# A hybrid decoder step on one core: normed rows kept in the operands' own buffers, all three thirds normed before the operand differences, and half of the down rows' low parts moved to VectorE

## The reference

```
hp = rms_norm(xp, norm_ffn[layer])
z = h @ w_up                      # 1024 -> 2 x 2816
g, u = split(z)
g_c, new_prev = causal_dwconv(g, prev, conv_w)        # width 3
xp = xp + (silu(g_c + conv_b) * u) @ w_down           # 2816 -> 1024
```

## Time and profile before

| | |
|---|---|
| median of 3 runs | 2657.35 us (2650.94 to 2659.35) |
| profiled execution | 2655.65 us |
| its span (first to last instruction) | 2653.9 us |
| mean granted TensorE clock | 0.967 of full speed |

### The profile page before, as it was taken

How to read it: one execution, slowest core, us unless ns; L and a number is a source line. 1 busy time by engine, 2 the same in 40 slices (tenths; PEclk the granted TensorE clock), 3 DMA queues, 4 the chain that set the end, 5 groups by cost and what they waited for, 6 DMA issues and landing times. The chain is left out here.

```text
span 2653.9 us, 43480 instructions
## 1 busy us (share of the span) xinstructions
PE 2478.8 (93%) x17818; PEld 2359.4 (89%) x17818; DVE 1532.3 (58%) x1863; ACT 823.7 (31%) x1304; POOL 1116.4 (42%) x752
## 2 busy tenths in 40 slices
PE   5999978999889999999999999879889999999997
PEld 4999955659889999999998999869889999999997
DVE  5988976533686666664447303172686666654446
ACT  4311144542343333332113322221343333332111
POOL 3766641002265555554443212252265555554441
PEclk9999988999989999999999999989989999999998
DMA  3887779993022222233220212312012322233221
GB/s 145 285 299 256 256 273 321 331 335 120 25 64 72 95 74 73 83 118 115 91 84 33 108 40 60 135 50 101 25 64 72 97 72 73 89 120 106 89 72 64
DMA packets 135185, 330.69 MB, mean 125 GB/s; under 512 B 21157, under 2 KB 25126, under 8 KB 134474
## 3 DMA queue, kind: packets, MB, share of 16 engines
q1 hardware_dynamic: 110634, 259.30, 28.4%
q10 hardware_dynamic: 24064, 67.56, 7.6%
q0 software_dynamic: 288, 1.05, 0.1%
HBM read 284.52 MB, written 43.32 MB: 124 GB/s over the span
## 5 line engine op out<-in xcount | busy, mean ns | idle before, releaser
L1396 PE MATMUL PS<-OP,OPW 128*128 128x258 f32 x7056 | 854.7, 284 | 18.8 <-DVE GUP L2633 7.4
L1396 PEld LDWEIGHTS PS<-OP,OPW 128*128 128x128 f32 x7056 | 853.1, 191 | 20.3 <-issue 15.2
L1031 PE MATMUL G<-HHI,WHI 128*128 128x344 f32 x2496 | 726.4, 323 | 23.7 <-POOL WLO L2843 12.1
L1031 PE MATMUL G<-HHI,WLO 128*128 128x344 f32 x2016 | 648.1, 321 | 0.0
L1031 PE MATMUL G<-HLO,WHI 128*128 128x344 f32 x1536 | 493.0, 321 | 0.0
L1031 PEld LDWEIGHTS G<-HHI,WHI 128*128 128x128 f32 x2496 | 460.0, 190 | 27.1 <-issue 26.3
L2843 POOL TENSOR_TENSOR WLO<-WRAW,WHI 128x1024 fp32r<-128x1024 f32 x94 | 231.5, 2469 | 563.9 <-ACT WHI L1636 563.8
L2505 DVE TENSOR_TENSOR XT<-XT,G 128x1032 f32<-128x1032 f32 x172 | 211.4, 1229 | 354.4 <-PE G L1031 354.1
L1031 PEld LDWEIGHTS G<-HHI,WLO 128*128 128x128 f32 x2016 | 382.6, 190 | 0.0
L2921 POOL TENSOR_TENSOR OPW<-WRAW,OPW 128x512 fp32r<-128x512 f32 x200 | 279.0, 1400 | 205.7 <-ACT OPW L1949 205.7
L1031 PEld LDWEIGHTS G<-HLO,WHI 128*128 128x128 f32 x1536 | 291.0, 189 | 0.3
(11 more groups left out here) (365 smaller groups left out, 3388.6 us busy)
## 6 DMA issues: line engine op xcount, KB each, us to landing
XT<-in_ck SPq DMA_DIRECT2D x256, 256.0 KB, 4.7
WRAW<-in_w ACTq DMA_DIRECT2D x108, 512.0 KB, 3.7
HF<-in_cv SPq DMA_DIRECT2D x176, 256.0 KB, 4.8
WRAW<-in_w SPq DMA_DIRECT2D x60, 512.0 KB, 4.0
hidden_rows<-HRB SPq DMA_DIRECT2D x44, 516.0 KB, 6.2
VTOK<-hidden_rows SPq DMA_DIRECT2D x22, 1032.0 KB, 4.9
XT<-in_cv SPq DMA_DIRECT2D x80, 256.0 KB, 4.5
SPARE<-in_w SPq DMA_DIRECT2D x22, 512.0 KB, 5.4
```

Of the source, the lines that this page charges most:

```text
L1031: mm = pe.matmul(out[:, c], w, x[:, c * TC:(c + 1) * TC], start=first and n == 0, stop=last and n == 2)
L1396: mm = pe.matmul(out[:, q * PIECE:(q + 1) * PIECE], w[:, at], v, start=starts and c == 0 and r == 0, stop=ends and c == 3 and r == 2, skip ...
```

## The change

1. `HNB` goes. Each normed row is written where later a difference is formed in place (`RAW1`, `RAW2`), so that all thirds can be held. For the middle third its place is in four runs, and `normed` writes it by two instructions of 172 columns instead of one of 344.
2. VectorE norms all three thirds first and then forms the differences (`operand_add`, in place, order T1, T3, T2, T4), between the weight sums. `conv_gate(0)` comes ahead of the low part of T1's last third, and all low parts of T4 after that.
3. ScalarE: GATE's copy no longer waits for the last difference, but the high parts of T2 now stand ahead of it; the copies of pair 1's P2 and P5 and the high parts of T3 stand ahead of SiLU 0, and the high parts of P4 and P7 behind it. GpSimd: all its low parts of third 1 ahead of P1's; the states of pair 0 ahead of P3's low part, T3's low parts ahead of P4's.
4. At the end of the pairs, ScalarE loads down unit 1 with unit 0 and rounds both together; GpSimd makes both units' low parts (unit 1's after P6 of the last pair) before the hidden rows.
5. VectorE makes the low part of every chunk's second hidden row (`second_low`): chunk 0's ahead of the last `conv_gate`, chunk c + 1's behind tile 3 of chunk c. GpSimd keeps the first rows. TensorE and SyncE wait for both counters.

Squares use another buffer (`SQ_FRONT`), and two semaphores are merged; neither adds a wait that is not there before.

```
         def normed_raw(n, b, c):
-            return HNB[:, c] if n % 2 else third(HN[c % 4], b)
+            if n % 2 == 0:
+                return third(HN[c % 4], b)
+            raw, size, apart = (RAW1, RAW1_SIZE, LOWER) if c < 4 else (RAW2, RAW2_SIZE, OPERAND)
...
+                    if n % 2 and b == 1:
+                        STT(out=out[:, 0], in0=x[:, 0], scalar=gain, in1=scale[:, 0], op0=ALU.mult, op1=ALU.mult)
+                        out, x, scale = out[:, 1], x[:, 1], scale[:, 1]
...
                 invert(n, 1)
-                operand_adds(n, 0)
                 normed(n, 1, 0, 4)
                 invert(n, 2)
                 normed(n, 1, 4, ND)
-                operand_adds(n, 1)
+                normed(n, 2)
+                operand_add(layer, X_T1, 0)
+                operand_add(layer, X_T1, 1)
                 weight_sum(layer, 1, S1)
+                operand_add(layer, X_T1, 2)
                 weight_sum(layer, 1, S3)
-                operand_low(layer, X_T4, 0)
-                normed(n, 2)
-                operand_adds(n, 2)
+                for x in (X_T3, X_T2, X_T4):
+                    operand_add(layer, x, 0)
                 operand_low(layer, X_T1, 0)
...
+                operand_low(layer, X_T1, 1)
...
                 weight_sum(layer, 1, S2)
                 weight_sum(layer, 1, S4)
...
+                conv_gate(0)
                 operand_low(layer, X_T1, 2)
-                conv_gate(0)
+                operand_low(layer, X_T4, 0)
...
+                def second_low(c):
+
+                    dve.wait_ge(hid_hi, layer * NF + 2 * c + 2)
+                    xhi, xlo = down_parts(c)
+                    TT(xlo[:, 1], HRAW[c % 2][:, 1], xhi[:, 1].bitcast(F32), ALU.subtract).then_inc(hid_lo_dve, 1)
...
+                    if p == NF - 1:
+                        second_low(0)
                     conv_gate(p)
...
                         add_tile(td + 8 * c, m, None)
+                        if m == 3:
+                            second_low(c + 1)
...
                 act.wait_ge(tile_done, tp + 2)
-                act.wait_ge(t_added, adds_count(layer, 2, X_T3))
                 A(by3(GATE), psum_tile(tp), ACT.Copy).then_inc(tile_free[tp % 2], 1)
-                turned_to_high(layer, 7, 8)
                 A(by3(HRB[:]), psum_tile(tp + 1), ACT.Copy).then_inc(tile_free[(tp + 1) % 2], 1)
+                turned_to_high(layer, 5, 6)
                 op_high(layer, 1, P6)
                 op_high(layer, 1, P3)
-                turned_to_high(layer, 8, 9)
+                turned_to_high(layer, 6, 9)
+                copy_product(1, P2)
+                turned_to_high(layer, 9, 11)
+                copy_product(1, P5)
+                turned_to_high(layer, 11, 12)
                 silu(0)
                 op_high(layer, 1, P4)
...
                         low(ud)
+                        pool.wait_ge(product_done, product_count(layer, p, P6))
+                        low(ud + 1)
                         hidden(0)
-                        low(ud + 1)
```

More of the change, by code:

```diff
@@ L1996, in mlp @@
                 act.wait_ge(tile_done, tp + 2)
-                act.wait_ge(t_added, adds_count(layer, 2, X_T3))
                 A(by3(GATE), psum_tile(tp), ACT.Copy).then_inc(tile_free[tp % 2], 1)
-                turned_to_high(layer, 7, 8)
                 A(by3(HRB[:]), psum_tile(tp + 1), ACT.Copy).then_inc(tile_free[(tp + 1) % 2], 1)
+                turned_to_high(layer, 5, 6)
                 op_high(layer, 1, P6)
                 op_high(layer, 1, P3)
-                turned_to_high(layer, 8, 9)
+                turned_to_high(layer, 6, 9)
[3 more added lines that the diff above has]
+                turned_to_high(layer, 11, 12)
                 silu(0)
                 op_high(layer, 1, P4)
[L2006 to L2012, removed]
+                op_high(layer, 1, P7)
+                op_high(layer, 2, P1)
+                op_high(layer, 2, P2)
+                for p in range(1, NF - 1):
+                    if p > 1:
                         op_high(layer, p + 1, P1)
@@ L2015, in mlp @@
                         op_high(layer, p + 1, P2)
[L2016 to L2043, removed]
+                        copy_product(p, P5)
+                    op_high(layer, p + 1, P5)
+                    op_high(layer, p + 1, P6)
+                    copy_product(p, P3)
+                    op_high(layer, p + 1, P3)
+                    copy_product(p, P4)
+                    op_high(layer, p + 1, P4)
+                    silu(p)
+                    op_high(layer, p + 1, P7)
+                p = NF - 1
+                act.wait_ge(op_lo_ready, product_count(layer, p - 1, P7))
+                load(ud)
+                load(ud + 1)
+                copy_product(p, P2)
+                copy_product(p, P5)
+                act.wait_ge(op_lo_ready, product_count(layer, p, P7))
+                load(ud + 2)
+                high(ud)
+                high(ud + 1)
+                copy_product(p, P3)
+                hidden(0)
+                copy_product(p, P4)
+                high(ud + 2)
+                load(ud + 3)
+                silu(p)
+                load(ud + 4)
                 for c in range(FI - 1):
@@ L2950, in mlp @@
                 n = 2 * layer + 1
-                pool.wait_ge(h_lo_pool, max(count for (m, b, c), (on, count) in LOWS.items() if m == n and on))
-                pool.wait_ge(h_lo_dve, max(count for (m, b, c), (on, count) in LOWS.items() if m == n and not on))
-                pool.wait_ge(t_added, adds_count(layer, 2, X_T3))
+                pool.wait_ge(h_lo_dve, LOWS[n, 2, 0][1])
                 nc.gpsimd.memset(GUP[:, 0:2], 0.0).then_inc(pool_const, 1)
```

155 lines of the change are left out of this document (86 added, 69 removed).

## The result

The changed kernel takes 2660.70 us (median of 20 runs, 2654.21 to 2666.99) against 2656.46 us (20 runs, 2649.31 to 2662.99): ratio 1.0018, 95% interval 1.0010 to 1.0026. It is slower by 4.2 us. That lies inside the predicted range and within 0.3%, but it is a loss that the measurement resolves, and the forecast was no change at all. The profiled execution of after took 2656.72 us (span 2654.8), only 1 us over the one of before, so the two traces have to be cut into stretches before they say anything.

A forecast was written before the change was run, and what follows sets the result against it. It took TensorE, busy 93% of the span, as the bound, with gains only where it waits for VectorE or GpSimd. Two layers of +2.3 - 2.3 summed to 0: 2655.6 us, range 2645 to 2664.

The forecast's parts named there:

- Thirds and P1: Start of a layer: no wait before third 2, P1 some 10 us sooner, near 1925, waited away before P2 and P5.
- P5 and P7: Pair 1 on TensorE: P5 near 1950.1 instead of 1944.90, P7 at 1968.1 instead of 1965.79, +2.3 us a layer.
- P5's sum: VectorE's list up to P5: differences +2.2, norm splits +1.4, convolution +4.0, T4's low parts -2.4; sum +5.2 us.
- eight splits: Middle third's norms halved on VectorE: 0.17 us fixed cost each, +1.4 in all, bounds 0 and 4.2.
- The table load: ScalarE before SiLU 0: the 1.28 us load, hidden at 1941.58 before, now stands on the path to P7.
- The step that failed: Twenty pairs behind P7: no long wait interrupts them, so the first stage is worth what it moves P7's start.
- The down start: Start of the down projection: wait of 6.06 shrinks to 0.4, tile 2 waits 4.4 us; -2.3 us a layer.
- The other ten second low parts a layer cost nothing either: Later down chunks: VectorE idles 1.60 us per tile, the part takes 1.23; without that cover 12 us a layer.
- The sum: Whole kernel: 2 x (+2.3 - 2.3) = 0 against the profiled 2655.65, so 2655.6 us.
- the wait at tile 2: Slower rival: the down start's wait moves to tile 2 and grows, +2.5 us a layer there, 2665.2 us; chance 0.12.
- its lower bound: Faster rival: VectorE waits less for GpSimd, P7 -3.0, down start -5.6 us a layer, 2638.5 us; chance 0.22.
- the down part: Third rival: hidden rows' load lands later, both ends of the down start cancel, 2660.2 us; chance 0.10.

The follow-up runs named there:

- e4: The changed kernel with the first SiLU and its table load right behind P2's copy; both layers took 1427.51 us against the changed kernel's 1430.54.
- e5: The changed kernel with pair 1's copy of P3 and second combine ahead of two weight sums; both layers 1422.60 us against 1430.54.
- e3: The kernel before with only the SBUF places of operands T2 and T4 exchanged; 2659.28 us against 2654.24, ratio 1.0018.
- e2: The changed kernel with its down-projection part undone, so norms-first and in-place operands alone; 2663.61 us against 2654.24 of the kernel before, ratio 1.0032.
- e9: The changed kernel with the copies that P2 waits for ahead of two of T2's high parts and T1's last; both layers 1433.38 us against 1430.54.
- e7: The kernel before with unit 1's load, high and low part earlier, all low parts of down rows left on GpSimd; ratio 1.0002.
- e13: The kernel of e7 timed a second time against the kernel before; ratio 0.9976, both layers 1420.78 us.
- e1: The kernel before with unit 1 earlier and VectorE making every second low part of the down rows; 2652.25 us against 2654.24, ratio 0.9984.
- e6: The changed kernel with the edits of e4 and e5 together; 2651.18 us against 2654.24 of the kernel before, ratio 0.9983.
- e10: e8 plus VectorE adding tiles between the last convolution's steps, its SiLU, gating and saving later; 2637.65 us against 2656.03 of the kernel before, ratio 0.9930.
- e8: e7 with pair 1's copy of P3 and second combine ahead of two weight sums; 2641.94 us against 2654.86 of the kernel before, ratio 0.9964.

## Why the prediction was wrong, point by point

- **Thirds and P1**: right. No wait before third 2, P1 at 1925.10 (near 1925), the 10 us waited away before P2 (13.83 us, some 14).
- **P5 and P7**: right in place, and in what each waits for: P5 at 1949.48 (1950.1), P7 at 1967.91 (1968.1). That P5's sum came so near is in part luck, since terms of it were off both ways. The halves of the norm run at a pace of 0.305 us (1906.85, 1907.16, 1907.46), two for one of 0.525, so eight splits cost 0.7 us a layer and not 1.4; the slope behind the 1.4 was taken between rows of two different operations. The convolution took 5.8 us (1942.67 to 1948.47) and not 4.0: its two steps of 8 columns took 1.14 and 1.28, where they took 0.23 each before. The other terms came out some 1.6 less in all; they were not taken apart. For the split, the estimate by the Trainium skill ("VectorE: DVE Perf Modes", The TRN2 errata) was 0.5, nearer than mine. Over both layers P7 came 2.55 us later in the mean.
- **The table load**: it stands where forecast, 1955.43. SiLU begins at 1956.73, 0.02 us behind the load's end, and ScalarE's operation ahead of the load ends at 1955.42, so the drain that the Trainium skill ("ScalarE: Activation LUTs", What ACT_TABLE_LOAD costs) adds to each switch does not show there. "Now it is on the path" was too simple: e4 shows that T3's high parts take its place when it leaves, and e5 that the path ends in the combine's place on VectorE.
- **The step that failed** is "Behind P7 come twenty pairs of products that no long wait interrupts, so the first stage is worth what it moves P7's start". That there is no wait was right; that the stretch is then the same was not: it is 1.64 us a layer longer. The diff's line of places was costed at nothing, without a word. Alone it slows the product matmuls by 0.3 ns in the mean, 1.0 to 1.2 us a layer (e3). Of the mean +1.64 the rest, 0.5, is half-speed time behind P7's wait, nearly all of it in layer 1; the prediction costed such time behind P5 and at the down start, but not here.

The view by stretches around P7 (columns as above). Of after, layers 0 and 1:

```profile
770.65:777.45 6.80, 5.59 (x34) 0.75 0.26 104
1966.70:1973.50 6.80, 5.59 (x26) 0.50 0.25 101
```

Of before, layer 1:

```profile
1966.90:1973.70 6.80, 6.80 (x46) 0.75 0.01 3
```

Behind the same wait of 4.41 us the clock is granted at the 1.2 GHz level through the whole stretch in layer 1 and for half of it in layer 0; before, behind 3.69 us, it is half of it. e2 repeats the two of after (407.43 and 408.62 us for the products), and e9, behind the same wait, has the longer time in both layers (408.47 and 408.35). So this 0.5 us does not follow from the wait's length alone, and what decides was not found.

- **The down start**: right on average (-1.53 and -3.25, mean -2.39, against -2.3), with the wait of 3.4 us at tile 2 where 4.4 was worked out. What the prediction put down to both parts together belongs to unit 1's order (e7, e13). "The other ten second low parts a layer cost nothing either" had a small miss, which the prediction named as a sign of being wrong: the part of chunk 1 held tile 6 in layer 0 (the third wait of the group DVE XT, 0.9 us: 7.8 in all less twice 3.4).
- **The sum**: +2.55 + 1.64 - 2.39 = +1.80 a layer, +3.6 in all. Two errors of the same sign that the forecast did not have, places (some 2.2 us for both layers) and half-speed behind P7 (1.0), are most of it; the 0.25 a layer on P7's start is the rest. None of the rivals came true: the wait at tile 2 stayed below the 4.4 us worked out for it, P7 did not come near its lower bound, and the down part did what it says.

## What to carry to other kernels

Cut a long trace at marks that both kernels share and compare stretches: here the part outside the layers differed by up to 16 us from one profile to another, four times the effect, while the layers of a kernel profiled twice repeated within 2 us. A diff's line that only moves data is an edit too; look at the matmuls done in a fixed length without waits. And the longest wait of TensorE is worth only the distance to the next thing that is late: 13.8 us here were worth nothing, 4.4 us behind a list in the wrong order were worth 4.6 to 5.1.

## What was not expected of the hardware

- The pace of the product matmuls changed when two of their operands exchanged places in SBUF: 2929 or 2930 against 2921 to 2923 of them in 350 us at clock 1.00, the same in both layers and in every kernel with the same places that was counted (before, e1; after, e2, e3, e6). Nearly all of it falls on P3, P4 and P7, two of which take operands that did not move. Which property of the addresses does it was not found, and other orders of the operands were not tried.
- The last convolution's steps beside GpSimd's low parts took 2.49 to 3.47 us (e7) where the same steps of the first convolution in e1 take 0.23 to 1.29. Work taken from GpSimd and given to VectorE at this place changed nothing (e1 against e7); work that need not stand there, put elsewhere, did (e10: the down stretches fell from 232.25 and 230.76 us in e8 to 227.70 and 228.12).
